# Hybrid encoder block: first inverses of the scan moved first, the output norm shared with GpSimd, a new order behind the scan

## What is computed

```python
def step(S, inp):
    rt, wt, kt, vt, at, bt = inp
    Sa = einsum('zbhij,zbhj->zbhi', S, at)
    S = S * wt[..., None, :] + Sa[..., :, None] * bt[..., None, :] + vt[..., :, None] * kt[..., None, :]
    return S, einsum('zbhij,zbhj->zbhi', S, rt)
y = ys[:, 0] + ys[::-1, 1]                      # both directions
mu, var = mean(y), mean((y - mu) ** 2)          # per head: the output norm
y = (y - mu) * rsqrt(var + LNX_EPS) * lnx_g + lnx_b
o_rwkv = (y + bonus) * (sigmoid(gd) @ gate_g2)
x = x + concatenate([o_rwkv, o_att]) @ w_out    # then a gated ConvFFN, and a last norm
```

## Time and profile before

| | |
|---|---|
| median of 3 runs | 1449.39 us (1448.84 to 1450.17) |
| profiled execution | 1443.46 us, span 1441.6 us |
| TensorE busy | 1313.0 us, 91% |
| VectorE busy | 872.8 us, 61% |
| ScalarE busy | 519.5 us, 36% |
| GpSimd busy | 223.2 us, 15% |
| scan, first to last state sum | 363.12 to 604.73 us |

### The profile page before, as it was taken

The page is one execution under the profiler, slowest core; times in us unless marked ns, Lnnn a source line. Parts: engine busy times, 40 slices in busy tenths (PEclk is TensorE's granted clock), DMA queues, the critical chain, the costliest instruction groups (busy, mean ns, idle before and its releaser), DMA issues.

```text
span 1441.6 us, 28459 instructions
## 1 busy us (share of the span) xinstructions
PE 1313.0 (91%) x11292; PEld 1029.2 (71%) x11292; DVE 872.8 (61%) x1071; ACT 519.5 (36%) x696; POOL 223.2 (15%) x229
## 2 busy tenths in 40 slices
PE   6999899894898988789968999999999999999996
PEld 2476677773666666557857888888888887888885
DVE  4977677896665787763358655555556573332235
ACT  3725425310354655542125333333333341121121
POOL 1000100130122221240101322222222200000000
PEclk9999999997697998899979999999999999999998
DMA  5046857884557766511410322222222256222113
GB/s 203 19 117 169 194 141 176 199 250 96 158 165 270 218 205 185 163 40 44 175 44 18 101 75 72 85 87 87 87 87 87 88 176 231 87 90 96 44 33 117
DMA packets 154788, 179.52 MB, mean 125 GB/s; under 512 B 61648, under 2 KB 117008, under 8 KB 154736
## 3 DMA queue, kind: packets, MB, share of 16 engines
q1 hardware_dynamic: 141568, 152.69, 35.8%
q10 hardware_dynamic: 9264, 14.19, 3.1%
q0 software_dynamic: 3904, 11.93, 2.6%
HBM read 121.16 MB, written 57.54 MB: 124 GB/s over the span
## 4 chain that ended last, share of the span: by engine, by line
PE 61%; issue 15%; DVE 13%; POOL 5%; DMA 2%; ACT 2%; SPq 1%; DVEq 0%; POOLq 0%; ACTq 0%
PE banks L1061 27%; PE banks L683 17%; PE banks L665 6%; PE banks L1096 5%; POOL work L1585 3%; PE banks L671 3%; DVE work L1839 2%; DVE work L1843 2%; PE banks L647 1%; DVE op L1637 1%; POOL h_lo L1600 1%; DVE work L1727 1%; DVE work L1724 1%; DVE hT L1660 1%; DVE hT L1979 1%
## 5 line engine op out<-in xcount | busy, mean ns | idle before, releaser
L1061 PE MATMUL banks<-op,sw_hi 128*128 128x512 f32 x1176 | 364.5, 391 | 4.5 <-DVE hT L2041 4.1
L1061 PEld LDWEIGHTS banks<-op,sw_hi 128*128 128x128 f32 x1176 | 222.0, 189 | 51.4 <-DVE sw_lo L1637 4.5
L1061 PE MATMUL banks<-op,sw_lo 128*128 128x512 f32 x588 | 229.7, 391 | 0.0
L1991 DVE TENSOR_TENSOR xT<-xT,banks 128x1024 f32<-128x1024 f32 x24 | 29.3, 1221 | 168.9 <-PE banks L683 157.2
L1061 PEld LDWEIGHTS banks<-op,sw_lo 128*128 128x128 f32 x588 | 111.1, 189 | 23.4
L1398 ACT ACTIVATE sw_hi<-work 128x1024 fp32r<-128x1024 f32 (+1 forms) x63 | 75.8, 1204 | 123.2 <-PE banks L1061 112.4
L1637 DVE TENSOR_TENSOR sw_lo<-work,sw_hi 128x1024 fp32r<-128x1024 f32 (+1 forms) x63 | 89.9, 1427 | 39.3 <-ACT sw_hi L1398 39.3
L665 PE MATMUL banks<-ph_hi,pw_hi 128*128 128x512 f32 x272 | 87.8, 405 | 6.2 <-DVE work L1757 2.2
L1585 POOL TENSOR_TENSOR work<-work 128x384 f32<-128x384 f32 x64 | 53.8, 871 | 238.7 <-DVE work L1891 238.7
L1611 POOL TENSOR_TENSOR work<-work 128x512 f32<-128x512 f32 x21 | 27.3, 1302 | 384.1 <-DMA work<-in_w_gu 298.0
L665 PE MATMUL banks<-ph_hi,pw_lo 128*128 128x512 f32 x272 | 86.0, 398 | 0.0
(11 more groups left out here) (246 smaller groups left out, 2488.2 us busy)
## 6 DMA issues: line engine op xcount, KB each, us to landing
work<-scan_d SPq DMA_DIRECT2D x32, 768.0 KB, 4.7
work<-in_w_gu SPq DMA_DIRECT2D x88, 256.0 KB, 4.5
scan_d<-work SPq DMA_DIRECT2D x16, 1024.0 KB, 5.4
g_d<-hT SPq DMA_DIRECT2D x22, 512.0 KB, 2.9
scan_d<-work SPq DMA_DIRECT2D x32, 256.0 KB, 6.5
work<-in_w_down SPq DMA_DIRECT2D x16, 512.0 KB, 3.8
work<-in_w_in ACTq DMA_DIRECT2D x15, 512.0 KB, 3.8
work<-g_d SPq DMA_DIRECT2D x15, 512.0 KB, 4.5
```

Source lines behind the costliest of these rows:

```text
L1061: mm = pe.matmul(banks[:, 3 * slot + bank, :], w[:, n, k * P:(k + 1) * P], x[n][:, k, :], start=(opens and k == 0 and p_ == 0), stop=(k == ...
L1991: tt(x, x, product, ALU.add).then_inc(added[slot], 1)
```

## The change

1. Of the moves of inverse rows, those for the first step (cc = 1) are issued first and counted apart. The stores of TI[1] to TI_d go from SP's and ScalarE's queue to GpSimd's. TensorE leaves out the first step's product with the zero state.
2. GpSimd's loop is cut anew (blocks 0; 1, 2; then pairs), so that the reload of x stands behind block 2 and not behind block 3.
3. In iterations 5 to 7 GpSimd makes the sum, the centring and, one iteration later than now, the scaling. VectorE keeps the means (q = 2), the sums of squares (q = 0 of the next iteration) and the reciprocals (q = 1). ScalarE squares at q = 3 and takes roots at q = 0 of the next iteration.
4. Behind the scan VectorE scales the last softmax block; TensorE makes the gates between probabilities and values, in ps[0] and ps[1] alone; VectorE makes the low parts of k = 5, 6 and 0 to 3, GpSimd those of 4 and 7; the products of k = 0 to 3 alternate between the two slots; and ScalarE's copies, squares and roots stand in another order.

Cut (unchanged bodies, GpSimd's operands as on VectorE; twelve leading spaces removed):

```diff
@@ -495,14 +498,10 @@
...
+for cc in (1, 0):
     for j in range(NPAIR):
         at = C * j + NC - 2 + cc
-        sp.dma_start(TIs[0][0:C, 1, cc, j, :], TI[1][at:at + 1, 0])\
-          .then_inc(scan_full[0] if j == 0 else s["lw_full"], 16)
...
-      .then_inc(s["TI1_stored"], 16)
+        sp.dma_start(TIs[0][0:C, 1, cc, j, :], TI[1][at:at + 1, 0]).then_inc(inverse_moved[1 - cc], 16)
 sp.wait_ge(s["TI1_stored"], 16 * 2 * NPAIR)
 load_inverses(1, 1)
@@ -903,18 +902,21 @@
         if lead and q == 0:
             pe.wait_ge(scan_full[slot], 16 * 8)
         elif cc == 0:
-            pe.wait_ge(scan_full[slot], 16 * 10 * i + 16 * 10)
+            pe.wait_ge(scan_full[slot], 16 * 10 * i + 16 * (10 - 2 * (slot == 0)))
...
+                if lead and q == 0 and j == NPAIR - 1:
+                    mm.then_inc(X_mm[z], 1)
+        if not (lead and q == 0):
+            pe.wait_ge(s["S_new"], n + 1)
+            settled()
+        for z, c2 in () if lead and q == 0 else enumerate(c2s):
...
-        if lead and q == 0:
-            pe.wait_ge(scan_full[0], 16 * 10)
-            pe.wait_ge(s["lw_full"], 16 * (NPAIR + 6))
-            pe.wait_ge(s["q_stored2"], 16 * 10)
+        if lead and q < 2:
+            pe.wait_ge(inverse_moved[q], 16 * 2 * NPAIR)
@@ -977,20 +977,29 @@
...
-for g in range(2):
-    probabilities(NC // 4 - 1, g, 8 * (NC // 4), range(3))
-    values(NC // 4 - 1, g, range(3), 8 * (NC // 4), vs_last, last_full)
...
+probabilities(NC // 4 - 1, 0, 8 * (NC // 4), range(3))
 pe.wait_ge(s["gw_loaded"], 16)
-pe.wait_ge(s["o_out"], 2 * NT + FREE)
 pe.wait_ge(s["Y_out"], NC + FREE)
 pe.wait_ge(s["S_add"], NC + FREE)
-for j in (2, 3, 0, 1):
-    whole(ps[j], gw[:, j * P:(j + 1) * P], sgT, s["gt_mm"])
+for j in range(2):
+    gate_product(j)
+values(NC // 4 - 1, 0, range(3), 8 * (NC // 4), vs_last, last_full)
+probabilities(NC // 4 - 1, 1, 8 * (NC // 4), range(3))
+pe.wait_ge(s["gt_out"], 1)
+gate_product(2)
+values(NC // 4 - 1, 1, range(3), 8 * (NC // 4), vs_last, last_full)
+pe.wait_ge(s["gt_out"], 2)
+gate_product(3)
+o_low = {4: (sp_s["att_lo"], KD + 1), 5: (sp_s["o_lo"], 1), 6: (sp_s["o_lo"], 2), 7: (sp_s["att_lo"], KD + 2),
+         0: (sp_s["o_lo"], 3), 1: (sp_s["o_lo"], 4), 2: (sp_s["h_lo"], 1), 3: (sp_s["h_lo"], 2)}
...
 for j in range(2):
+    pe.wait_ge(s["gt_out"], 3 + j)
...
-for slot in range(2):
-    split_dense(ps[2 + slot], slot, o_hi, o_lo, KD,
-                ((0, sp_s["att_lo"], KD + NPAIR + 1), (1, sp_s["att_lo"], KD + NPAIR + 2), (2, sp_s["h_lo"], 1),
-                 (3, sp_s["h_lo"], 2)), (0, 1, 2, 3), opens=False)
+for k in range(NPAIR):
+    for slot in range(2):
+        split_dense(ps[2 + slot], slot, o_hi, o_lo, KD, ((k, *o_low[k]),), (k,), opens=False,
+                    closes=(k == NPAIR - 1))
@@ -1259,13 +1268,10 @@
...
-for cc in range(2):
+for cc in (1, 0):
...
-        act.dma_start(TIs[0][64:64 + C, 1, cc, j, :], TI[1][at:at + 1, 1]).then_inc(s["q_stored2"], 16)
-for j in range(NPAIR):
-    act.dma_start(TI_d[1, 1][:, :, j].rearrange("s c t -> c s t"), TI[1][C * j:C * (j + 1), 1])\
-       .then_inc(s["TI1_stored"], 16)
+        act.dma_start(TIs[0][64:64 + C, 1, cc, j, :], TI[1][at:at + 1, 1]).then_inc(inverse_moved[1 - cc], 16)
@@ -1305,14 +1311,14 @@
...
-            late = first == YT
+            late, again = first >= YT, first > YT
...
             if late and q == 3:
                 for b in range(2):
-                    y_root(2 * i + (b - 2 * YT), b)
+                    y_square(2 * i + (b - 2 * YT), b)
...
             if first == 0 and q == 0:
+                for moved in inverse_moved:
+                    act.wait_ge(moved, 16 * 2 * NPAIR)
...
-            if late and q in (1, 2):
-                y_square(2 * i + (q - 1 - 2 * YT), q - 1)
+            if again and q == 0:
+                for b in range(2):
+                    y_root(2 * i + (b - 2 * YT - 2), b)
@@ -1343,11 +1352,6 @@
...
-transposed(2 * (NC // 4) - 2, range(3))
-attended(NC // 4 - 1, 0)
-transposed(2 * (NC // 4) - 1, range(3))
-attended(NC // 4 - 1, 1)
...
-    act.activation(gates[:, j, :], ps[j], ACT.Copy).then_inc(s["gt_out"], 1)
...
+    act.activation(gates[:, j, :], ps[j % 2], ACT.Copy).then_inc(s["gt_out"], 1)
...
+transposed(2 * (NC // 4) - 2, range(3))
+for b in range(2):
+    y_root(NT - 4 + b, b)
 act.wait_ge(s["S_new"], NC + 1)
-for slot in range(2):
-    weights_hi(slot, 0)
+weights_hi(0, 0)
+gate_out(0, 1)
+gate_out(1, 2)
+attended(NC // 4 - 1, 0)
+transposed(2 * (NC // 4) - 1, range(3))
+y_square(NT - 2, 0)
+attended(NC // 4 - 1, 1)
 act.wait_ge(s["o_out"], 2 * NT + FREE)
-for k in range(NPAIR, KD):
-    act.activation(h_hi[:, k, :], oT[:, k, :], ACT.Copy).then_inc(sp_s["att_hi"], 1)
-gate_out(2, 1)
-gate_out(3, 2)
-for b in range(2):
-    y_square(NT - 2 + b, b)
-gate_out(0, 3)
-gate_out(1, 4)
+attention_hi(4)
+y_square(NT - 1, 1)
+attention_hi(5)
+weights_hi(1, 0)
+gate_out(2, 3)
+attention_hi(6)
+attention_hi(7)
 for b in range(2):
     y_root(NT - 2 + b, b)
+gate_out(3, 4)
@@ -1575,6 +1591,10 @@
...
 pool.wait_ge(s["sol_row"], 2 * (C - 1))
+for j in range(NPAIR):
+    for e in range(2):
+        pool.dma_start(TI_d[1, e][:, :, j].rearrange("s c t -> c s t"), TI[1][C * j:C * (j + 1), e])\
+            .then_inc(s["TI1_stored"], 16)
@@ -1585,23 +1605,54 @@
...
-for first, last in ((0, 2), (2, NC // 4)):
+def y_sum(m, r, slot, again):
+    pool.wait_ge(y_full[slot], 16 * r)
+    if again:
+        pool.wait_ge(s["y_var"], m + -1)
+    pool.tensor_tensor(ysum[slot], yin[slot][:, 0], yin[slot][:, 1], ALU.add).then_inc(yin_used[slot], 1)
...
+def y_centre(m, slot, again):
+    pool.wait_ge(s["y_chain"], 2 * m + 2)
...
+    pool.tensor_tensor(heads(ycen[slot]), heads(ysum[slot]), stat[slot][:, 0].unsqueeze(2).broadcast_to([P, AH, HD]),
...
+def y_normalise(m, tile, slot):
+    pool.wait_ge(s["y_inv"], m + 1)
...
+normalised(0, 0)
+for first, last in ((1, 2), (2, YT), (YT, YT + 1), (YT + 1, NC // 4)):
+    late, again = first >= YT, first > YT
     with pool.Fori(first, last) as i:
-        for g in range(2):
-            normalised(2 * i + g, g)
-    if first == 0:
+        if late:
+            for b in range(2):
+                y_sum(2 * i + (b - 2 * YT), i + (1 - YT), b, again)
+        normalised(2 * i + -1, 1)
+        if again:
+            y_normalise(2 * i + (-2 * YT - 2), i * -1 + (NC // 4 + 1), 0)
+            y_normalise(2 * i + (-2 * YT - 1), i + -2, 1)
+        if late:
+            for b in range(2):
+                y_centre(2 * i + (b - 2 * YT), b, again)
+        normalised(2 * i, 0)
+    if first == 1:
         pool.wait_ge(s["Y_mm"], 8)
         for k in range(KD):
             pool.dma_start(xT[:, k, :], a["xT"][:, k, :]).then_inc(s["x_again"], 16)
-for k in range(NPAIR, KD):
+for b, tile in enumerate((1, NC // 4 - 2)):
+    y_normalise(NT - 4 + b, tile, b)
...
     pool.tensor_tensor(h_lo[:, k, :], oT[:, k, :], h_hi[:, k, :].bitcast(F32), ALU.subtract)\
-        .then_inc(sp_s["att_lo"], 1)
-for j in range(2):
-    pool.wait_ge(sp_s["h_hi"], j + 1)
-    pool.tensor_tensor(h_lo[:, j, :], oT[:, j, :], h_hi[:, j, :].bitcast(F32), ALU.subtract)\
         .then_inc(sp_s["att_lo"], 1)
@@ -1891,17 +1942,28 @@
...
+def y_mean(m, r, slot):
     dve.wait_ge(yin_used[slot], r + FREE)
     dve.tensor_reduce(stat[slot][:, 0], heads(ysum[slot]), AX.X, ALU.add).then_inc(s["y_chain"], 1)
     dve.wait_ge(s["y_chain"], 2 * m + 1)
     ts(stat[slot][:, 0], stat[slot][:, 0], 1.0 / HD, None, ALU.mult).then_inc(s["y_chain"], 1)
...
+def y_inverse(m, slot):
+    dve.wait_ge(s["y_sd"], m + 1)
+    dve.reciprocal(stat[slot][:, 3], stat[slot][:, 2]).then_inc(s["y_inv"], 1)
...
-for first, last in ((0, 1), (1, YT), (YT, NC // 4)):
...
+            late, again = first >= YT, first > YT
...
                 logits(i, g, (0,), earlier)
+                for b in range(2):
+                    if again and q == 0:
+                        y_variance(2 * i + (b - 2 * YT - 2), b)
+                    elif late and q == 2:
+                        y_mean(2 * i + (b - 2 * YT), i + (1 - YT), b)
...
-            if late and q == 2:
-                y_variance(2 * i - 2 * YT, 0)
-            elif late and q == 3:
-                y_variance(2 * i + (1 - 2 * YT), 1)
             dve.wait_ge(s["S_mm"], n + 1)
+            if first == 0 and q == 0:
+                dve.wait_ge(s["S_new"], 1)
...
-            if late and q in (1, 2):
-                y_centre(2 * i + (q - 1 - 2 * YT), i + (1 - YT), q - 1)
-            elif late and q == 3:
-                y_normalise(2 * i - 2 * YT, i * -1 + NC // 4, 0)
-                y_normalise(2 * i + (1 - 2 * YT), i + -1, 1)
+            if again and q == 1:
+                for b in range(2):
+                    y_inverse(2 * i + (b - 2 * YT - 2), b)
+for b in range(2):
+    y_variance(NT - 4 + b, b)
 sums(2 * (NC // 4) - 1)
-for slot in range(2):
-    y_centre(NT - 2 + slot, NT // 2, slot)
+dve.wait_ge(s["inv_chain"], 4 * (NC // 4))
+for h in range(GH):
```

(28 more changed lines are left out.)

54 lines of the change are left out of this document (31 added, 23 removed).

## The result

| | changed | before |
|---|---|---|
| median | 1433.65 us (4 runs, 1428.01 to 1436.25) | 1449.12 us (4 runs, 1444.14 to 1450.17) |
| ratio | 0.9896, interval 0.9865 to 0.9927 | |
| profiled execution | 1435.67 us, span 1433.6 us | 1443.46 us, span 1441.6 us |

The forecast was 1429.7 us, with a range of 1418 to 1442. The kernel became 1.0% faster: 15.7 us against the median shown ahead of the prediction, where 19.7 were forecast. The two profiled executions differ by only 8, since that of before lies at the lower end of its kernel's times and that of after at the upper end of its own.

What follows compares the result with a forecast made beforehand. TensorE was taken to carry most of the span, waiting in the scan on its round with VectorE and ScalarE. Start -4.1, reload 0, late iterations -8.2 and behind the scan -7.4 took 1449.4 to 1429.7 us, range 1418 to 1442.

Steps and rivals of the forecast that it cites:

- start: Start of the scan: with the stores on GpSimd's queue ScalarE copies X earlier; -4.1 us, between -1 and -4.9.
- late iterations: Scan iterations 5 to 7: moving norm work off VectorE cuts the excess over the pace; -8.2 us, between -13.5 and -2.
- reload: GpSimd's loads of x in the scan start some 10 us earlier, TensorE's stall only moves; 0 us, between -3 and +4.
- behind the scan: After the last state sum: earlier softmax, low parts and gating, and reordered output products; -7.4 us, between -3 and -11.
- so the copy can start at 353.65: Scan start: ScalarE's X copy follows its eight moves directly once the stores leave its queue, 4.94 us earlier.
- Some 2 us of slack follow: Scan start: slack between step 0's Y copy and the next X copy; waiting for stores charged 0.3 us, at most 2.
- The stall moves and stays: Reload of x: it meets the load for steps 10 and 11 instead of 12 and 13; 0 us.
- rival B: Late iterations: GpSimd's queue becomes the wait as y lands later; 1439 us if mild (chance 0.03), 1457 if severe (0.04).
- late iterations stay at 32 us or more: Sign that the forecast is wrong, through port or queue; 28 to 31 us were expected per late iteration.
- Two scales, the state products L1951 of two steps and the row-sum update are the ones on the path: Late iterations: five VectorE operations may meet GpSimd's work, some 0.57 us each; 2.0 us taken, 1.3 in iteration 5.
- Rival A: The port shared by VectorE and GpSimd eats the late gain, 1.30 us per meeting: -8.5 us, 1441 us; chance 0.12.
- Rival C: The edit behind the scan does nothing; exponentials, y load and ScalarE's copies set the end: -12.3, 1437 us; chance 0.10.

Runs made afterwards that it cites:

- the stores back: Changed kernel with the eight stores of the second inverse back on SP's and ScalarE's queues, behind the moves: 1436.73 us, ratio to before 0.9902.
- both orders that brought the X copy forward: Changed kernel, GpSimd's stores waiting for all moves (1437.01 us), or for the first step's eight, with four moves shifted from ScalarE to SP (1434.57 us).
- the order back: Changed kernel with the output products of k = 0 to 3 run slot by slot again: 1437.48 us, ratio to before 0.9911.
- undoing part 3: Changed kernel with the output norm of iterations 5 to 7 on VectorE again: 1440.01 us, ratio to before 0.9939.
- undoing the low parts: Changed kernel with the low parts of the first two gated head pairs on GpSimd again: 1440.10 us, ratio to before 0.9938.

## Why the prediction was right, and where it was not

It was right in sign and within its range. The sum is 4 us too good beside the medians. By the table's pieces, the start, the late iterations and the reload together fell short of their terms by 7.9 us, and the work behind the scan gave 2.6 us more than its term, of which 1.6 us are luck.

| term | predicted | measured |
|---|---|---|
| start | -4.1 | 0 (second sum 370.58 against 370.70; the kernel with the stores back 0.7 ± 1.5 quicker at equal clock) |
| reload | 0 | +1.5 by the traces, not clear of nothing |
| late iterations | -8.2 | -5.9 ± 1.3 by the runs, -3.1 in the two traces |
| behind the scan | -7.4 | -10.0 |
| together | -19.7 | -14.4 (0 + 1.5 - 5.9 - 10.0, from runs and traces mixed); medians -15.7; at equal clock -13.9 ± 1.0 |

**Start.** The step that failed is "so the copy can start at 353.65". I priced the moves by their row of before, which had no other transfer beside it, and charged the stores only for the landing (0.5 us). They slowed the issue itself, 0.61 to 1.37 us each, and it is the issue that holds ScalarE. Also, the gain would not have lasted: "Some 2 us of slack follow" was read for stores that take 10.5 us from 348.5; they took 13.1, and in both orders that brought the X copy forward the Y copy waited for them. The Trainium skill (DMA: Bandwidth & Descriptors, section Issuing engines are not separate DMA queues) says that transfers interleave on the same 16 engines whoever starts them, and that another engine saves only issue time. This case agrees on the first (the moves landed after 4.3 instead of 1.8 us beside the stores) and adds that a third queue can cost issue time on the other two. That the stores cause it is shown by the two edits that take them away from the moves; by what means they do it is not.

**Reload.** "The stall moves and stays" held; what the early place may cost, 1.5 us, lies inside the bounds of -3 and +4.

**Late iterations.** The direction held, and GpSimd's queue was not the wait (rival B): in no trace does TensorE, VectorE or ScalarE wait for GpSimd between 510 and 604 us. The means cost what was priced: in iteration 6 VectorE's copy of U comes behind them at 557.88, 1.97 us after ScalarE's (priced at 1.9). The sign "late iterations stay at 32 us or more" came for one of the two whole ones (29.95 and 32.75 us), and it pointed at the port rightly, but the clock, which it did not name, had a share. The step at fault is "Two scales, the state products L1951 of two steps and the row-sum update are the ones on the path". The costliest meeting was not in that list: the three operations on 4 columns at the end of the second step (L1928 to L1932), which the prediction does not name. They cost 1.5 us (10.14 against 8.64) in iterations 6 and 7 when y lands at once. And the price of a meeting was mis-sized: not 0.57 us, but what is left of GpSimd's operation, up to nearly all of it. Rival A's rule, the Trainium skill's exclusive lock (SBUF — State Buffer, section Who interferes with whom), is what the rows show: 0.15 us becomes 1.23 beside a sum of 1.4, and 1.23 becomes 3.42 beside a low part of 2.40. What it is worth depends on who meets whom, so rival A's time, 1441, was not reached. The third steps, 8.0 to 10.7 us in iterations 6 and 7 where the pace is 6.27 and where the sum had at most a meeting, are a further part of the shortfall; before had 9.50 there as well.

**Behind the scan.** All steps stood in the order given: +25.9 for the first pair (+26.6 predicted), 1.23 us for each gated product (1.25), +40.5 for the last low part (+41.9). The stall for slot 0's weights is 1.49 us (1.3). The end is +112.1 (+114.6): 1.4 us come from the earlier low part and 1.1 from the work behind it, 71.6 us instead of 72.7, in which a group of six took 1.37 and not 1.396. For the same reason the gain over before is not all the change's. Of the 10.0 us, six groups fewer are 8.2 and the opening of the chain 0.15; the other 1.6 are luck, since in the trace of before TensorE ran at half speed from about 652.6 to 655.6 (granted clock 0.52), just behind the last low part, and the price per group was read from that row. With the order back, 324 matmuls took 73.80 us at full speed, not 75.39. Rival C is out.

What is left open: why undoing part 3 costs 5.9 us in the runs and 3 in one trace of each, and undoing the low parts 4.7 ± 1.3 in the runs and 2.1 in the trace. From L722 (L723 before) to the end of the span the traces take between 711.0 and 716.0 us at unchanged code: 714.3 in the changed kernel's and 711.0 in that of before. So some 3 us of the gain are missing between the two profiled executions in code that nothing changed. Behind the scan only the low parts and the order of the products were undone by themselves. The new softmax scaling, gates and order on ScalarE, by which the first pair comes 5.3 us earlier, were seen in the two traces alone.
